# Storing each expert item's result as one block from ScalarE's queue, and letting every token gather its two rows by index

## The reference

```python
def hier_moe(h, ...):
    g_p, g_idx = lax.top_k(softmax(t @ w_group + b_group), 1)       # one of 4 groups
    e_top, e_idx = lax.top_k(e_sel, 2)                              # two of its 8 experts
    e_w = softmax(e_top) * g_p
    ...
        gate, up = split(einsum('td,edf->tef', t, w_gate_up[gi]))   # 1024 -> 2 x 256
        act = silu(gate) * up * combine[:, gi, :, None]
        y = y + einsum('tef,efd->td', act, w_down[gi])              # 256 -> 1024
x = x + g2 * hier_moe(...)
```

## Time and profile before

| what | value |
|---|---|
| median of the three timed runs | 1552.93 us (1550.99 to 1553.7) |
| profiled execution: its own time | 1554.65 us |
| profiled execution: its span | 1552.9 us |
| busy: PE, weight load, DVE, ACT, POOL | 1383.2, 922.8, 726.1, 433.9, 406.1 us |
| mean granted TensorE clock | 0.944 of full speed |

### The profile page before, as it was taken

The page is one execution under the profiler, slowest core; times in us unless marked ns, Lnnn a source line. Parts: engine busy times, 40 slices in busy tenths (PEclk is TensorE's granted clock), DMA queues, the critical chain, the costliest instruction groups (busy, mean ns, idle before and its releaser), DMA issues.

```text
span 1552.9 us, 25844 instructions
## 1 busy us (share of the span) xinstructions
PE 1383.2 (89%) x9279; PEld 922.8 (59%) x9279; DVE 726.1 (47%) x1526; ACT 433.9 (28%) x1017; POOL 406.1 (26%) x609
## 2 busy tenths in 40 slices
PE   4999998999999895999988699999999959999881
PEld 2877776677887644554544287776774445555440
DVE  3555556355655337642222524555556376422224
ACT  3334234242444211000000445555543110000002
POOL 3132021020222001343423333344420022444320
PEclk9799999999999996999989889999999969999996
DMA  8253643443113336899999703211118169999995
GB/s 352 96 190 136 218 185 142 167 159 109 55 55 141 117 122 243 354 419 424 422 421 419 285 29 122 83 68 68 68 68 312 75 247 365 420 421 422 421 405 196
DMA packets 56696, 350.32 MB, mean 226 GB/s; under 512 B 18409, under 2 KB 18881, under 8 KB 30993
## 3 DMA queue, kind: packets, MB, share of 16 engines
q1 hardware_dynamic: 44992, 332.02, 53.9%
q0 software_dynamic: 11520, 16.83, 3.0%
q10 hardware_dynamic: 80, 0.04, 0.0%
HBM read 342.45 MB, written 27.34 MB: 238 GB/s over the span
## 4 chain that ended last, share of the span: by engine, by line
PE 71%; DMA 17%; DVE 7%; ACT 2%; issue 2%; SPq 0%; ACTq 0%; POOL 0%; DVEq 0%; POOLq 0%
PE PS L989 8%; PE PS L746 7%; DMA hT<-in_moe_w_down_dram 7%; PE PS L748 7%; PE PS L747 7%; PE PS L937 5%; PE PS L996 4%; DMA Dr<-in_ada_w_dram 4%; DMA Dr<-in_moe_w_down_dram 3%; PE PS L829 3%; PE PS L848 3%; PE PS L717 3%; PE PS L845 2%; PE PS L1016 2%; PE PS L1006 2%
## 5 line engine op out<-in xcount | busy, mean ns | idle before, releaser
L746 PE MATMUL PS<-hHi,Whi 128*128 128x512 f32 x512 | 228.2, 446 | 4.3 <-issue 4.2
L1231 ACT COPY arena<-PS 128x512 f32<-128x512 f32 (+3 forms) x256 | 112.4, 458 | 337.9 <-PE PS L829 180.9
L748 PE MATMUL PS<-hHi,Wlo 128*128 128x512 f32 x512 | 203.7, 398 | 0.0
L747 PE MATMUL PS<-hLo,Whi 128*128 128x512 f32 x512 | 203.0, 396 | 0.0
L989 PE MATMUL PS<-Wr,arena 128*64 128x256 f32 x1408 | 166.6, 391 | 5.0 <-DVE arena L2003 4.8
L2212 POOL TENSOR_TENSOR Wlo<-Wr,Whi 128x512 fp32r<-128x512 f32 (+1 forms) x80 | 104.7, 1325 | 190.8 <-ACT Whi L1231 189.8
L989 PEld LDWEIGHTS PS<-Wr,arena 128*64 128x64 f32 x1408 | 102.3, 141 | 83.9 <-issue 30.7
L1437 ACT ACTIVATE arena<-PS 128x128 f32<-128x128 f32 x72 | 20.0, 277 | 470.6 <-PE PS L989 391.4
L2267 POOL DMA_INDIRECT y_rows<-arena x72 | 74.8, 1039 | 251.7 <-DVE arena L2015 239.3
L746 PEld LDWEIGHTS PS<-hHi,Whi 128*128 128x128 f32 x512 | 98.2, 192 | 36.2 <-issue 22.1
L748 PEld LDWEIGHTS PS<-hHi,Wlo 128*128 128x128 f32 x512 | 97.6, 191 | 22.4
(11 more groups left out here) (357 smaller groups left out, 2419.1 us busy)
## 6 DMA issues: line engine op xcount, KB each, us to landing
Wr<-in_moe_w_gate_up_dram SPq DMA_DIRECT2D x52, 2048.0 KB
Dr<-in_ada_w_dram SPq DMA_DIRECT2D x42, 1024.0 KB, 27.1
Dr<-in_moe_w_down_dram SPq DMA_DIRECT2D x28, 1024.0 KB
arena<-in_moe_w_gate_up_dram SPq DMA_DIRECT2D x14, 2048.0 KB
hT<-in_moe_w_down_dram SPq DMA_DIRECT2D x26, 1024.0 KB
Wr<-in_gdn_w_dram SPq DMA_DIRECT2D x8, 2048.0 KB, 8.2
Wr<-in_fox_w_dram SPq DMA_DIRECT2D x8, 2048.0 KB, 7.8
shift_scale<-in_moe_w_down_dram SPq DMA_DIRECT2D x12, 1024.0 KB
```

The lines of the kernel that those rows point to most:

```text
L746: mm(out_ap, a_hi, b_hi, start=(k == 0), stop=False)
L747: mm(out_ap, a_hi, b_lo, start=False, stop=False)
L748: return mm(out_ap, a_lo, b_hi, start=False, stop=(k == KD - 1))
L1231: return nc.scalar.copy(dst, src)
```

## The change

Before, an item's 128 half rows were scattered by POOL, one indirect DMA per item, to the places of their tokens, and the combine read whole tiles. Now ACT stores `yo[u]` as it is, with two plain DMAs of 64 rows of 2 KB, to the item's own block of `y_items` (row `e * 64`), whether a place holds a row or not. A table `slot_y` says for each token in which row of `y_items` its two results lie; POOL gathers them at the end, with eight indirect DMAs of 128 rows of 4 KB. The table `slot_i` and two of the operations that made it are gone; four small ones make `slot_y`. The rows of the further items are filled once with finite values, by three loads on SP's queue in the DeltaNet stage. The name in the diff for `yo` stored by halves is `store_halves`; `store(e, u)` waits for `result(e)`.

```diff
-        y_rows = [nc.dram_tensor(f"y_rows{i}", (4 * T, D // 2), F32, kind="Internal").ap() for i in range(2)]
+        y_items = nc.dram_tensor("y_items", ((NI + MORE) * C, D), F32, kind="Internal").ap()
...
+            for r in range(NI * C, (NI + MORE) * C, T):
+                n = min(T, (NI + MORE) * C - r)
+                load(y_items[r:r + n, :], x[0, 0:n, :], y_filled)
             first_out_load()
...
-            def combine_load(i):
-                sp.wait_ge(M["done"], i + 1)
-                for u in range(2):
-                    sp.wait_ge(M["y"][u], 8 * NI * (i + 1))
-                for n in range(NT):
-                    for k in range(2):
-                        load(Y[k][:, n, :], y_rows[i][2 * (k * T + n * P):2 * (k * T + n * P + P), :].rearrange("(p h) c -> p (h c)", h=2),
-                             y_in[n])
...
+                def store(e, u):
+                    act.wait_ge(m["yo"], e + (B + 1))
+                    store_halves(e * C, u, m["y"][u])
+
+                def store_halves(row, u, landed):
+
+                    for g in range(2):
+                        act.dma_start(y_items[ds(row, C), 512 * g:512 * g + 512], yo[u][C * g:C * g + C, :]).then_inc(landed, 16)
+
                 def step(e, q):
                     silu(e, q % 2)
                     if not isinstance(e, int) or e >= 1:
                         act_turned(e - 1, (q + 1) % 2)
+                    if not isinstance(e, int) or e >= 2:
+                        store(e - 2, q % 2)
...
                 act_turned(NI - 1, 1)
-
+                store(NI - 2, 0)
                 log_exp_tables()
+                store(NI - 1, 1)
...
+                cpv(slot_b, slot_p)
...
+                link(TT(slot_d, slot_p, slot_b, ALU.subtract))
+                link(STT(out=slot_d, in0=slot_d, scalar=float(C * NI), in1=over_p, op0=ALU.add, op1=ALU.mult))
+                TT(slot_y, slot_d, slot_b, ALU.add)
...
-                cpv(slot_i[:, cs], slot_f[:, cs])
-                link(TS(slot_t[:, cs], slot_f[:, cs], 2 * T - 0.5, float(-2 * T), ALU.is_ge, ALU.mult))
-                TT(slot_g[:, cs], slot_f[:, cs], slot_t[:, cs], ALU.add).then_inc(idx_ok, 1)
+                cpv(slot_g[:, cs], slot_f[:, cs]).then_inc(idx_ok, 1)
...
                     if y_n is not None:
-                        dve.wait_ge(m["y"][u], y_n + 8 * B)
+                        dve.wait_ge(m["y"][u], y_n + 16 * B)
                     TT(yo[u], PS[6 + u][:], gate_halves, ALU.mult).then_inc(m["yo"], 1)
...
-                for q in range(4):
-                    put(NI - 4 + q, q, 16 * (NI // 2 - 2 + q // 2))
...
+                pool.wait_ge(y_filled, 16 * (-(-MORE * C // T)))
+                for u in range(2):
+                    pool.wait_ge(m["y"][u], 16 * NI * (i + 1))
+                    pool.wait_ge(more_y[u], so_far(pairs, i, n_p) * 32 + 32)
+                    passed()
+                for n in range(NT):
+                    for k in range(2):
+                        g.indirect_dma_start(out=Y[k][:, n, :], out_offset=None, in_=y_items,
+                                             in_offset=bass.IndirectOffsetOnAxis(ap=slot_y[:, k * NT + n:k * NT + n + 1], axis=0),
+                                             bounds_check=(NI + MORE) * C - 1, oob_is_err=False).then_inc(y_in[n], 16)
```

More of the change, by code:

```diff
@@ L317, in build @@
         slot_t = cv(NI + MORE)
-        slot_i = cv(NI + MORE, dt=I32)
+        slot_y = cv(2 * NT, dt=I32)
+        slot_b, slot_d = cv(2 * NT), cv(2 * NT)
         slot_g = cv(NI + MORE, dt=I32)
@@ L397, in build @@
         hr_out = sems("hr_out", 2)
[L398 removed]
+        y_in = sems("y_in", NT)
         slots_ps = sem("slots_ps")
         fin_ok = sem("fin_ok")
[L402 removed]
+        M = {n: sem(f"moe_{n}") for n in ("xt_ps", "xt", "gu_ps", "sg", "ac", "at_ps", "at", "dn_ps", "yo", "cp_g")}
         M["xg"] = sems("moe_xg", 4)
         M["y"] = sems("moe_y", 2)
[L405 to L407 removed]
+        y_filled = sem("y_filled")
         more_pe, more_dve, more_act = sem("more_pe"), sem("more_dve"), sem("more_act")
@@ L1478, in experts @@
                             cp(acT[u], PS[4][:, 0:P]).then_inc(more_act, 1)
+                        for u in range(2):
+                            act.wait_ge(more_dve, jj * 6 + (5 + u))
+                            store_halves(j * (2 * C) + (u + NI) * C, u, more_y[u])
                 with act.Else():
@@ L2264, in gather @@
                                          bounds_check=2 * T - 1, oob_is_err=False).then_inc(landed, 16)
-                def scatter(u, at, landed):
-                    g.indirect_dma_start(out=y_rows[i], out_offset=bass.IndirectOffsetOnAxis(ap=sidx[:, at, :], axis=0),
-                                         in_=yo[u], in_offset=None, bounds_check=4 * T - 1,
-                                         oob_is_err=False).then_inc(landed, 16)
                 def take(e, u):
@@ L2282, in take_again @@
                     take(e + 4, q)
-                def put(e, q, y_n):
-                    u = q % 2
-                    if y_n is not None:
-                        pool.wait_ge(m["y"][u], y_n + 8 * B)
-                        passed()
-                    g.tensor_copy(sidx[:, u, :], slot_i[:, ds(e, 1)]).then_inc(m["cp_s"], 1)
-                    pool.wait_ge(m["cp_s"], e + (B + 1))
-                    pool.wait_ge(m["yo"], e + (B + 1))
-                    passed()
-                    scatter(u, u, m["y"][u])
                 for e in range(4):
@@ L2298, in experts @@
                 take_again(0, 0)
-                put(0, 0, None)
                 pool.wait_ge(idx_ok, 4 * i + 3)
-                take_again(1, 1)
-                put(1, 1, None)
-                take_again(2, 2)
-                put(2, 2, 16)
-                take_again(3, 3)
-                put(3, 3, 16)
+                for e in range(1, 4):
+                    take_again(e, e)
                 with pool.Fori(1, NI // 4 - 1) as j:
@@ L2341, in experts @@
                             gather_more(j + 1, u)
-                            pool.wait_ge(more_cp[i], j * 4 + (u + 3))
+                            pool.wait_ge(more_cp[i], j * 2 + (u + 3))
                             passed()
                             gather(u, more_xg[i][u])
-                        for u in range(2):
-                            scatter_more(j, u)
-                            pool.wait_ge(more_cp[i], j * 4 + (u + 5))
-                            pool.wait_ge(more_dve, jj * 6 + (5 + u))
-                            passed()
-                            scatter(u, 2 + u, more_y[u])
-                        for u in range(2):
-                            pool.wait_ge(more_y[u], jj * 16 + 16)
-                        pool.sem_inc(more_free, 1)
                     for u in range(2):
@@ L2357, in experts @@
                     pool.nop()
-                pool.sem_inc(m["done"], 1)
+                pool.wait_ge(y_filled, 16 * (-(-MORE * C // T)))
+                for u in range(2):
+                    pool.wait_ge(m["y"][u], 16 * NI * (i + 1))
[6 more added lines that the diff above has]
+                                             bounds_check=(NI + MORE) * C - 1, oob_is_err=False).then_inc(y_in[n], 16)
             g.memset(plan[:, 2, :], 0.0)
```

25 lines of the change are left out of this document (8 added, 17 removed).

## The result

The changed kernel took 1582.94 us (median of 4 runs, 1571.93 to 1590.94); the kernel before took 1551.96 us beside it (4 runs, 1549.6 to 1553.7). The ratio is 1.0195, 95% interval 1.0161 to 1.023: slower, clear of noise. The profiled execution took 1580.28 us with a span of 1578.2 us, against 1552.9 before, at a mean granted clock of 0.940 against 0.944.

A forecast was written before the change was run, and what follows sets the result against it. DMA engines' bytes bound both mixture layers up to their deciding weight loads, then serial tails. 10.8 + 12.6 - 0.6 + 2.2 - 1.3 = +23.7 us on 1554.65 gives 1578.3; median 1.72 lower, 1576.5; range 1564 to 1594.

The forecast's parts named there:

- Bytes, +23.4: Up to both layers' deciding weight loads, stores of every place add DMA time over scatters: +10.8 and +12.6 us.
- The wait for `yo`, 0: Mid-layer, stores land before `result` needs the buffer again; a landing of up to 10.1 us costs nothing: 0.
- The rival of late stores: Mid-layer, stores land in 12.2 us, stretching each item from 6.1 to 6.8 us: 43 us, total 1596; chance 0.13.
- PE's waits for down weights "up from 13.3 to about 24 us": Layer 0, sign in the changed profile that the forecast is right; unchanged waits would mean stores are free.
- `result` waiting for `y_items` in mid-layer: Mid-layer, sign in the changed profile that the forecast is wrong and stores land late.
- Layer 0's tail, gain 1.5: From layer 0's last results to the combine's first rows, a shorter path: gain 0.2 to 4.3 us, 1.5 taken.
- The subtractions, +3.7: Layer 0's combine: POOL's eight subtractions now run beside it, costing 0 to 9.8 us; three waits of 1.23 us taken.
- lock through all eight: Layer 0's combine: DVE is held through all eight subtractions, +6.1 us on the forecast, 1583; counted within the forecast.
- Layer 1's tail, -1.3: From layer 1's last result to DVE's combine, store plus gathers take 8.7 instead of 10.03 us: -1.3.
- The index tables, -0.6: Ahead of each layer's first gather, two small operations fewer: -0.3 us a layer; making `slot_y` costs 0.
- Free stores: Both layers: HBM writes run beside weight reads, so the scatters' 10.1 + 10.8 us go: 1532; chance 0.07.
- The change does less than it says: In the stores, bytes of empty places are not moved; nothing there could leave them out. No size or separate chance given.

The follow-up runs named there:

- e3_half_bytes: The changed kernel with each store covering only the first 256 of 512 elements of a row, same number of DMAs; 1566.25 us, ratio 1.01.
- e4_no_bytes: The changed kernel with each store covering only the first 16 of 512 elements of a row, same number of pieces; 1550.78 us, ratio 0.9997.
- e6_early_late: The changed kernel with POOL's eight subtractions behind the combine and each store issued ahead of the next item's SiLU; 1571.28 us, ratio 1.0131.
- e1_lo_late: The changed kernel with POOL's eight subtractions waiting until layer 0's combine is through; 1576.14 us, ratio 1.0164.
- after: The changed kernel itself, with the whole change and nothing else, against the kernel before; 1582.94 us, ratio 1.0195.
- e2_before_lock: The kernel before with POOL's eight subtractions delayed to lie beside layer 0's combine; 1553.57 us, ratio 1.0015.
- e10_gather_late: The kernel before, scatters kept, with the combine's rows fetched by eight indirect POOL gathers and the subtractions behind the combine; 1558.53 us, ratio 1.0032.

## Why the prediction was right, step by step

The forecast was 1576.5 us, the median 1582.94, within the range and with the sign. The mechanism, bytes in a stretch that the DMA engines bound, is shown by e3_half_bytes and e4_no_bytes. The median lies 6.4 us above the forecast. Several terms were off, and partly cancelled, so that the number is closer than its terms:

- **Bytes, +23.4: the two layers grew by 20.7** (11.3 and 9.4). Some 2 to 5 us of this are not bytes but late landing (e6_early_late), so the bytes alone are 16 to 18. The step that was off is the price of 2.66 us for a megabyte of stores: up to the deciding loads e4_no_bytes stores 16.0 MB less and is 34.5 us shorter, 2.2 us a megabyte. For the scatters the price was nearer: their 7.8 MB cost the 13.8 us and what late landing costs in e4_no_bytes, so 1.8 us a megabyte at least, and 2.0 to 2.4 if that is the 2 to 5 us of above (an estimate). The low end, 18.2, with the weights' price for the stores, was nearer.
- **The wait for `yo`, 0: measured 2.4 us in layer 0**, and up to 2.5 in layer 1, which is within that layer's spread. The landing that was bounded by 2.6 and 7.61 us took 8.3 us in the median of e1_lo_late and 9.83 us in after's chain; the rows showed no plain store beside full engines. The slack of 10.1 us was not tested by itself. The rival of late stores put the landing at 12.2 us, the time of an item at 6.8 and the cost at 43 us. It was right early in a layer: from item 2 to item 13 an item takes 6.8 and 7.0 us in after, 6.4 before. It was wrong over the whole of it, where the wait for weights covers most of this.
- **PE's waits for down weights "up from 13.3 to about 24 us": wrong**, 11.7 us. By that mark the text would have read the stores as free. The mark "`result` waiting for `y_items` in mid-layer", given for late stores, came true with 81.9 us, and the forecast held all the same. The added time is idle time in pieces too small for the list; the layer's length and PE's busy time show it, a single wait does not.
- **Layer 0's tail, gain 1.5: measured 0.3 to 0.6**. A shorter way for the last result (its store landed in 3.64 us) against a gather of 6.79 us where 3.6 was taken.
- **The subtractions, +3.7: measured +10.2** in three of three profiles with all bytes and the subtractions in after's place. This was just outside the bounds (0 to 9.8) and was the rival "lock through all eight" at 1583, which the median hits by coincidence with the terms above. In the medians the subtractions weigh less: after's ratio is 1.0195 and 1.0219 in two groups of runs, e1_lo_late's 1.0164, a difference of 5 to 9 us, with intervals that overlap or touch (1.0161 to 1.023 and 1.0189 to 1.025 against 1.0137 to 1.019). The prediction took the row of 4.14 us to be in line with a lock that lasts for one operation; it spans more than three subtractions and is rather the first sign of a longer hold. The turns that I had taken as the likely case exist (e2_before_lock, +4.0), but not in the changed kernel as it stands.
- **Layer 1's tail, -1.3: measured +3.4, and +0.8 behind it**. Result to store took 5.8 us (1545.21 to 1550.98) where 3.7 was taken, and from there to the first addition 7.7 us (at 1558.65) where 5.1 was. The gather's time was taken from layer 0's first gather on quiet engines and 0.6 us were added for its bytes; the chain shows 6.22 us. Eight gathers also start 1.30 us apart, not 1.05. The sign was wrong: in layer 1 the gathers alone cost 2.0 us in e10_gather_late's step (12.7 against 10.7), and 5.0 us in its median over both layers.
- **The index tables, -0.6; ScalarE's issue, 0; the fill, 0**: nothing that the runs could tell from 0. The stage ahead of layer 0 varies by 10 us from run to run. ScalarE's issue took 0.48 us a DMA. The fill's three DMAs landed before the engines had work again.
- **Not foreseen**: FoX took 380.3 to 380.6 us in the three profiles with all bytes and a held addition, and 377.7 to 378.5 us in the three with the subtractions moved. But e4_no_bytes has 377.3 us with a held addition and e10_gather_late 380.8 with moved subtractions, so no cause is named.
- **Free stores** fell: 18 MB of stores cost 34.5 us. **The change does less than it says** fell too: q10 moved all of its 18.92 MB.

The medians can be split as follows, in us above before: gathers alone 5.0 (e10_gather_late); bytes on top 15.3 (e6_early_late has 20.3); late landing 5.1 (e1_lo_late less e6_early_late, 0.0033 of 1552); held addition 4.8 to 8.5; together 30 to 34. Each term is the difference of two runs that follow each other in the list, so they add up to after's ratios by construction, and the sum proves nothing. The milestones, which are read from single profiles, give 2.8 us for late landing. No version beat the kernel before: the best of the changed ones, e6_early_late, is 1.31% slower, and e4_no_bytes shows that even without nearly all of its stores' bytes the change only draws level.

## What to carry to other kernels

Where the DMA engines are full, count what a change moves there, in bytes: a store of all places in place of a scatter of those that exist pays for each empty one. Before taking an indirect load for a plain one, look at what else its engine does next: here POOL's gathers pushed eight subtractions from an idle time into the combine, which only the order of instructions shows. A window of fixed times compares two kernels only where it lies at the same place in the work. And a landing time should be taken from a transfer under the same load, or its upper bound put well above the longest row.

## What the runs showed of the hardware

- DVE and GpSimd, both with two SBUF inputs: an addition of 1.28 us and subtractions of 1.23 us either took turns (2.2 to 2.3 us an addition, 13.8 to 15.8 us for eight subtractions) or the addition was held for all eight (10.4 to 11.4 us). The Trainium skill, "SBUF — State Buffer", section on who interferes with whom, says that a DVE instruction with two SBUF inputs contends with a GpSimd instruction that reads SBUF. Of DVE's modes that use both port pairs it says that whoever issues first gets the shared pair for the whole instruction and the other fully blocks. Turns agree with such a lock. The held ones do not in full: the addition waited through eight instructions, four times after having started 0.2 to 0.5 us ahead of the first.
- Plain stores of 128 KB took 8.3 us in the median of e1_lo_late, whose engines are full for most of them, and 9.83 us in after's chain, and 3.64 us in 868 to 872 us, where the engines' share was down to 0.33. Beside full engines the size hardly mattered: stores of 4 KB took 7.9 us in the median of e4_no_bytes.
- With the engines full (418 to 424 GB/s in all), 16.0 MB less of stores made the two layers 34.5 us shorter, 2.2 us a megabyte: stores are not free beside loads here.
- Indirect gathers of 128 rows of 4 KB were issued every 1.30 us and landed in a median of 6.0 us; SP's plain loads of the same size took 6.7 but started closer together (0.43 us to issue). So what the gathers lose is in the spacing and the start, not in one gather's landing.
